# Prompt softmax of a hybrid decoder step: semaphores counted per head, and one move for both heads' turned weights where they fit in one bank

## The chip, the cores and the metric

The kernel runs on one core of one Trainium2 chip. The metric is device time in microseconds. Three runs of the kernel before gave 2883.32 to 2887.96 us, with a median of 2884.73 us.

## The reference

Two layers of a decoder step, for a prompt of 512 tokens and 8 sample requests of one token, each with 1024 cached tokens in pages of 128. Each layer normalizes, projects, attends, merges the branches by sigmoid gates and ends with a SwiGLU FFN. The attention has three kinds: native sparse attention (compressed, selected and window branch), stick-breaking, and forgetting attention (FoX). What the change touches is the masked softmax of the prompt:

```
def masked_softmax(s, mask):
    s = jnp.where(mask, s.astype(jnp.float32), NEG_INF)
    e = jnp.where(mask, jnp.exp(s - jnp.max(s, axis=-1, keepdims=True)), 0.0)
    return e / jnp.maximum(jnp.sum(e, axis=-1, keepdims=True), 1e-30)

p_c = masked_softmax(einsum('btghd,bngd->bghtn', qg, ck) * scale, c_mask);  o_c = einsum('bghtn,bngd->btghd', p_c, cv)
p_w = masked_softmax(einsum('btghd,bsgd->bghts', qg, k_win) * scale, w_mask); o_w = einsum('bghts,bsgd->btghd', p_w, v_win)
o = g[..., 0:1] * o_c + g[..., 1:2] * o_s + g[..., 2:3] * o_w
```

With 512 tokens, the selected and the window branch see every earlier token, so their weights form a causal triangle, as FoX's do. The compressed branch has 31 keys.

## The kernel before, in words

Each engine has its own program, and semaphores order them. A layer is `norm`, `project`, `compress`, `attend`, `merge`, `norm`, `ffn`. The change lies in `attend`, whose order is one list, `PLAN`, built by `in_order()` (from line 113). TensorE, VectorE and ScalarE each walk this list and skip what is not theirs; POOL walks `ITEMS` alone.

**Items.** `SOFT` has 14 units: for each of four pairs of query heads "cmp", "sel" and "win", then two units "fox". Each unit has four items, one for each block of 128 query rows (i = 0 to 3), so `ITEMS` has 56, numbered n. An item works on two heads, hh = 0 and 1. Its width w is 31 columns for "cmp" and (i + 1) x 128 otherwise. One item passes through these steps:

- `scores` (TensorE, lines 759 to 768): the scores of both heads go to PSUM banks 0 and 1. From n = 1 on it first waits for `exp_done` n, the exponentials of the item before.
- `scores` (VectorE, line 1700): the negated maximum of both heads.
- `exponentials` (ScalarE, line 1338): one operation for each head with the row sum as a by-product, into the buffer `Pb[:, n % 2]`; the semaphore rises after the second.
- `weigh` (VectorE, lines 1709 to 1713): mask, sum and clamp for "cmp" only, then the reciprocals of both heads' sums in one operation.
- POOL (lines 1492 and 1495): each head's weights times its reciprocal and its gate; `p_scaled` rises after the second head.
- `turn` (TensorE, line 582): for each head i + 1 transposes of 128 x 128 (one of 31 columns for "cmp") into bank 2. Head 0 waits for `p_scaled` and for VectorE's move of the item before; head 1 goes to the same columns of the bank and waits for ScalarE's move of head 0.
- `turn` (ScalarE, lines 1349 and 1351, head 0; VectorE, lines 1723 and 1725, head 1): the move from bank 2 to `PTb` in SBUF.
- `values` (TensorE, lines 800 and 802): after the fourth item of a unit, weights times values into bank 3.

The list has scores(n + 1), turn(n, 0), turn(n, 1), exp(n + 1), weigh(n + 1), and so on. On ScalarE the move of head 0 of item n is therefore ahead of the exponentials of item n + 1, and on VectorE the order is maximum of n + 1, move of head 1 of n, reciprocals of n + 1.

**Cached pages.** Between these parts `in_order()` spreads the work on the samples. Up to item 41 these are mostly the key pages: `turn_s` (four transposes, TensorE, also line 582, from the tile `units`), their move by VectorE (line 1788) and `score_s` (lines 938 and 939). Then come the samples' own softmax (lines 1796 to 1829, ScalarE 1388 to 1398) and, spread over the prompt items that are left and the stick-breaking heads, `value_s` (lines 1006 to 1009). SyncE loads the pages (`load_unit`, lines 541 and 557) into six slots in a fixed order; a slot is free when TensorE has read what was in it. The value pages of request b + 1 wait in this way for `value_s` of request b.

After the items follow the four stick-breaking heads; the first waits for the last exponentials and the last move of the softmax.

Of the kernel before, what the change touches and what calls it, by code (L numbers as in the profile page):

```python
# [13 lines left out]
P = 128  # L14
# [33 lines left out]
CONST, _c = {}, 0  # L48
# [36 lines left out]

STEPS = ([(("selk", b, 0), ("selk", b + 4, 0), j) for b in range(4) for j in range(2)]
# [89 lines left out]
def layer_counts():  # L176
# [9 lines left out]
             s_ps=items, nm_ready=items, exp_done=items, rr_ready=items, p_scaled=items, pt_ps=2 * items,  # L186
             pt_ev_a=items, pt_ev_d=items, pv_done=2 * len(SOFT), o_ev=8,
# [11 lines left out]
def build(nc, A, out):  # L199
# [4 lines left out]
    with ctx:  # L204
# [373 lines left out]
        def _(pe):  # L578
# [168 lines left out]
            def scores(l, n):  # L747
# [4 lines left out]
                if n >= 1:  # L752
                    pe.wait_ge(sems["exp_done"], at(pe, "exp_done", l, n))
# [16 lines left out]

            def turn(l, n, hh):

                u, i = ITEMS[n]
                if hh == 0:
                    pe.wait_ge(sems["p_scaled"], at(pe, "p_scaled", l, n + 1))
                    if n >= 1:
                        pe.wait_ge(sems["pt_ev_d"], at(pe, "pt_ev_d", l, n))
                else:
                    pe.wait_ge(sems["pt_ev_a"], at(pe, "pt_ev_a", l, n + 1))
                if SOFT[u][1] == "cmp":  # L780
                    last = tp(ps[0:NCP, 2, 0:P], Pb[:, n % 2, hh, 0:NCP], P)
                else:
                    for j in range(i + 1):
                        last = tp(ps[:, 2, j * P:(j + 1) * P], Pb[:, n % 2, hh, j * P:(j + 1) * P], P)
                last.then_inc(sems["pt_ps"], 1)

            def values(l, u):
                idx, br = SOFT[u]
                n = u * TT + TT - 1
                pe.wait_ge(sems["pt_ev_a"], at(pe, "pt_ev_a", l, n + 1))  # L790
                pe.wait_ge(sems["pt_ev_d"], at(pe, "pt_ev_d", l, n + 1))
# [17 lines left out]
            def stick(l, hd):  # L809
# [4 lines left out]
                if hd == 0:  # L814
                    pe.wait_ge(sems["exp_done"], at(pe, "exp_done", l, len(ITEMS)))
                    pe.wait_ge(sems["pt_ev_d"], at(pe, "pt_ev_d", l, len(ITEMS)))
# [405 lines left out]
        def _(act):  # L1222
# [107 lines left out]
            def exponentials(l, n):  # L1330
# [6 lines left out]
                for hh in range(2):  # L1337
                    last = fn(Pb[:, n % 2, hh, 0:w], ps[:, hh, 0:w], ACT.Exp, bias=nm[:, n % 2, hh:hh + 1], accum_out=sm[:, n % 2, hh:hh + 1])  # L1338
                last.then_inc(sems["exp_done"], 1)

            def turn(l, n, hh):
                if hh:
                    return
                u, i = ITEMS[n]
                act.wait_ge(sems["pt_ps"], at(act, "pt_ps", l, 2 * n + 1))
                if i == 0 and u >= 1:
                    act.wait_ge(sems["pv_done"], at(act, "pv_done", l, 2 * u))
                if SOFT[u][1] == "cmp":
                    fn(PTb[0:NCP, 0, 0, i * P:(i + 1) * P], ps[0:NCP, 2, 0:P], ACT.Copy).then_inc(sems["pt_ev_a"], 1)
                else:  # L1350
                    fn(PTb[:, 0, 0:i + 1, i * P:(i + 1) * P], ps[:, 2, 0:(i + 1) * P].rearrange("p (j c) -> p j c", c=P), ACT.Copy
                       ).then_inc(sems["pt_ev_a"], 1)
# [126 lines left out]
        def _(pool):  # L1479
            with pool.Fori(0, DEPTH) as i0:  # L1480
                l = in_layers(pool, i0)
                for n, (u, i) in enumerate(ITEMS):
# [13 lines left out]
                    last.then_inc(sems["p_scaled"], 1)  # L1496
# [62 lines left out]
        def _(dve):  # L1559
# [142 lines left out]
            def weigh(l, n):  # L1702
# [3 lines left out]
                dve.wait_ge(sems["exp_done"], at(dve, "exp_done", l, n + 1))  # L1706
                if SOFT[u][1] == "cmp":
                    m = CONST["cmp01"][0] + i * 32
                    link(v.tensor_tensor(Pb[:, b, :, 0:NCP], Pb[:, b, :, 0:NCP],
# [392 lines left out]
```

## Time and profile before

| | |
|---|---|
| median of 3 runs | 2884.73 us (2883.32 to 2887.96) |
| the profiled execution | 2888.6 us |
| its span, first to last instruction | 2886.8 us |
| mean granted TensorE clock | 0.935 of full speed |
| attention, layer 0 | from about 318 us to about 760 us |
| attention, layer 1 | from about 1728 us |

The profile gives, for each engine, the time in which it was busy, and for each instruction how long the engine had stood idle before it and which instruction of which engine ended that. An entry such as "PE ps L582 <- POOL ring L1495" reads: TensorE's instruction of line 582, which writes the tile ps, waited for POOL's instruction of line 1495, which writes the tile ring. `Pb` and `PTb` are parts of the tile ring, so the transposes of the prompt's weights are those of line 582 with input "cst,ring", and the page transposes those with "cst,units". The number of transposes in a row (x1 to x4) tells the row block i.

### The profile page before, as it was taken

Reading aid. Unit: us, or ns where it says so; the run is one execution under the profiler, and the core shown is the slowest. Engines: PE = TensorE matmul, PEld = TensorE weight load, DVE = VectorE, ACT = ScalarE, POOL = GpSimd, SP = SyncE. Lnnn points to the kernel's source line nnn. Section 1 sums busy time; section 2 is a strip of 40 time slices with the busy share of each in tenths; the row PEclk is TensorE's granted clock in tenths of the full one; section 3 lists DMA queues with packets and bytes.
Section 4 is the critical chain, followed back from the end, with each engine's and each line's share of the span. In section 5 each row is a group of like instructions: output and inputs, shape, how many; then the busy total and the mean of one; then the engine's idle time right before and its main releaser. Section 6 shows DMA issues by size and latency. Waiting matters only on the chain.

```text
span 2886.8 us, 43032 instructions
## 1 busy us (share of the span) xinstructions
PE 2584.5 (90%) x13546; PEld 1991.7 (69%) x13546; DVE 897.1 (31%) x1801; ACT 538.7 (19%) x1356; POOL 638.0 (22%) x564
## 2 busy tenths in 40 slices
PE   5997788877899999999999878888689999999997
PEld 4885544444588878888888664444357887888886
DVE  2203455421222432233131145552112334223412
ACT  1013222212222111110010232222141220111100
POOL 0000012111132424443300001121111242444431
PEclk8999789877999999999999998997789999999998
DMA  6242334245122212222514233341532222222120
GB/s 190 82 127 73 91 103 120 72 117 156 67 88 88 88 59 88 88 70 71 161 52 137 62 105 100 110 125 40 171 101 88 87 79 68 87 82 83 64 81 30
DMA packets 288295, 270.89 MB, mean 94 GB/s; under 512 B 50882, under 2 KB 249746, under 8 KB 287810
## 3 DMA queue, kind: packets, MB, share of 16 engines
q1 hardware_dynamic: 271266, 258.43, 29.2%
q10 hardware_dynamic: 16800, 9.61, 1.1%
q8 instruction: 119, 1.95, 0.3%
q14 instruction: 110, 0.90, 0.1%
HBM read 258.36 MB, written 17.97 MB: 96 GB/s over the span
## 4 chain that ended last, share of the span: by engine, by line
PE 77%; SPq 8%; issue 5%; DVE 5%; ACT 2%; POOL 1%; DMA 1%; ACTq 0%; DVEq 0%; POOLq 0%
PE ps L1042 32%; PE ps L1163 8%; PE ps L582 6%; PE ps L648 5%; PE ps L649 5%; SPq L557 3%; PE ps L938 3%; PE ps L863 2%; PE ps L802 2%; SPq L554 2%; POOL ring L1495 1%; PE ps L759 1%; PE ps L614 1%; PE ps L613 1%; PE ps L716 1%
## 5 line engine op out<-in xcount | busy, mean ns | idle before, releaser
L1495 POOL TENSOR_SCALAR ring<-ring,rr,gnat 128x31 f32<-128x31 f32 (+2 forms) x192 | 100.6, 534 | 1063.8 <-DVE rr L1713 1063.8
L1042 PE MATMUL ps<-hT,ring 128*128 128x260 f32 x1344 | 307.2, 386 | 8.2 <-DVE hT L1597 8.2
L1042 PEld LDWEIGHTS ps<-hT,ring 128*128 128x128 f32 x1344 | 258.2, 192 | 49.4 <-DVE hT L1597 9.0
L582 PE MATMUL ps<-cst,units 128*128 128x128 f32 x960 | 161.3, 302 | 61.2 <-ACT arena L1314 16.8
L1042 PE MATMUL ps<-hT,units 128*128 128x260 f32 x928 | 213.2, 382 | 0.0
L648 PE MATMUL ps<-hT,ring 128*128 128x260 f32 x672 | 202.4, 383 | 0.0
L649 PE MATMUL ps<-hT,ring 128*128 128x260 f32 x672 | 202.1, 382 | 0.0
L1042 PEld LDWEIGHTS ps<-hT,units 128*128 128x128 f32 x928 | 176.3, 190 | 27.1
L582 PEld LDWEIGHTS ps<-cst,units 128*128 128x128 f32 x960 | 114.6, 152 | 103.9 <-ACT arena L1314 38.0
L582 PE MATMUL ps<-cst,ring 128*128 128x128 f32 (+1 forms) x464 | 104.7, 314 | 75.9 <-POOL ring L1495 36.8
L1042 PE MATMUL ps<-arena,units 128*128 128x260 f32 x704 | 157.9, 382 | 0.0
L582 PEld LDWEIGHTS ps<-cst,ring 128*128 128x128 f32 (+1 forms) x464 | 54.9, 147 | 138.6 <-issue 72.5
L1042 PEld LDWEIGHTS ps<-arena,units 128*128 128x128 f32 x704 | 133.8, 190 | 20.5
L1788 DVE COPY arena<-ps 128x512 f32<-128x512 f32 x176 | 120.0, 687 | 88.4 <-PE ps L582 86.6
L649 PEld LDWEIGHTS ps<-hT,ring 128*128 128x128 f32 x672 | 127.7, 190 | 19.6
L648 PEld LDWEIGHTS ps<-hT,ring 128*128 128x128 f32 x672 | 126.3, 191 | 18.3
L1532 POOL TENSOR_TENSOR units<-ring 128x512 f32<-128x512 f32 x44 | 59.8, 1358 | 338.4 <-PE ps L1042 338.4
L1510 POOL TENSOR_TENSOR units<-ring 128x512 f32<-128x512 f32 x32 | 40.5, 1267 | 385.5 <-PE ps L1042 270.8
L1441 ACT ACTIVATE arena<-ps 128x260 f32<-128x260 f32 x132 | 51.1, 387 | 362.5 <-PE ps L1042 362.5
L1006 PE MATMUL ps<-units,arena 128*32 128x256 f32 x256 | 87.9, 506 | 33.2 <-DMA units<-in_cache_sb_kv 25.6
L1700 DVE TENSOR_REDUCE nm<-ps 128x2 f32<-128x256 f32 (+2 forms) x112 | 72.8, 650 | 140.4 <-PE ps L768 132.9
L1338 ACT ACTIVATE ring<-ps,nm 128x128 f32<-128x128 f32 (+2 forms) x224 | 100.3, 454 | 21.7 <-DVE nm L1700 21.2
(319 smaller groups left out, 4381.5 us busy)
## 6 DMA issues: line engine op xcount, KB each, us to landing
ring<-in_w_in SPq DMA_DIRECT2D x20, 2048.0 KB, 7.9
units<-in_cache_fox_kv SPq DMA_DIRECT2D x256, 128.0 KB, 2.2
units<-in_cache_sb_kv SPq DMA_DIRECT2D x256, 128.0 KB, 2.2
ring<-in_w_ffn_gate SPq DMA_DIRECT2D x22, 1024.0 KB, 5.4
ring<-in_w_ffn_up SPq DMA_DIRECT2D x22, 1024.0 KB, 8.0
ring<-in_w_ffn_down SPq DMA_DIRECT2D x16, 1408.0 KB, 6.2
units<-in_cache_nsa_cmp_kv SPq DMA_DIRECT2D x128, 128.0 KB, 2.6
units<-in_cache_nsa_sel_kv SPq DMA_DIRECT2D x256, 64.0 KB, 1.8
```

The costliest lines, as they stand in the source:

```text
L557: dma(slot[:, j * cols:(j + 1) * cols], rows(name)[l * NPOOL + pg][:, c0:c0 + cols]).then_inc(sem, 16)
L582: return nc.tensor.transpose(o, i, ident[0:n, 0:n])
L648: mm(ps[:, 2 * (i % 2), 0:H2], w[:, k, j * P:(j + 1) * P], hT[:, k, 0:H2], start=k == 0, stop=k == KD - 1)
L649: last = mm(ps[:, 2 * (i % 2) + 1, 0:H2], w[:, k, j * P:(j + 1) * P], hT[:, k, H2:T], start=k == 0, stop=k == KD - 1)
L938: mm(ps[lo, bank, :], qa, KT[0][:, i % 2, :], start=first, stop=True, skip_group_check=True).then_inc(sems["smm_a"], 1)
L1006: fox = mm(bank[64:96, 0:256], PTf[:, 4 * h + j, :], sf[:, j, :], start=h == 0 and j == 0, **sk)
L1042: last = mm(ps[:, bank, 0:H2], w[:, k, :], a[:, k, :], start=first and k == 0, stop=True, skip_group_check=True)
L1163: last = mm(ps[:, bank, 0:H2], w[:, k, :], x[k] if x is D2 else x[:, k, :], start=first and k == 0, stop=True, skip_group_check=True)
L1338: last = fn(Pb[:, n % 2, hh, 0:w], ps[:, hh, 0:w], ACT.Exp, bias=nm[:, n % 2, hh:hh + 1], accum_out=sm[:, n % 2, hh:hh + 1])
L1495: last = nc.gpsimd.tensor_scalar(p, p, one, gnat[:, i, c:c + 1], ALU.mult, ALU.mult)
L1700: v.tensor_reduce(nm[:, n % 2, :], ps[:, 0:2, 0:w], AX.X, ALU.max, negate=True).then_inc(sems["nm_ready"], 1)
L1788: v.tensor_copy(KT[s][:, i % 2, :], bank).then_inc(sems["kt_ev"], 1)
```

## The change

`exp_done`, `rr_ready` and `p_scaled` count heads instead of items. ScalarE raises `exp_done` after each head's exponentials. VectorE takes a reciprocal for each head by itself, except for "cmp", where it still takes both in one operation and raises the semaphore by two. POOL waits for each head's reciprocal and raises `p_scaled` after each head. TensorE's turn waits for the scaling of its own head.

A function `joint(n)` is true for "cmp" items and for i = 0 and 1. There both heads' turned weights lie side by side in bank 2, TensorE does not wait between them, and one instruction moves both: ScalarE's where n is even, VectorE's where n is odd. For i = 2 and 3 of the other branches head 0 is moved by ScalarE and head 1 by VectorE into and out of the same columns, as before. `MOVED_A` and `MOVED_D` hold how many moves each engine has made before item n. Before it overwrites or reads what was moved, TensorE waits for both counts.

```diff
+def joint(n):
+    u, i = ITEMS[n]
+    return i < 2 or SOFT[u][1] == "cmp"
+
+MOVED_A, MOVED_D = ([sum(not joint(m) or m % 2 == d for m in range(n)) for n in range(len(ITEMS) + 1)] for d in range(2))
...
+        def turned_weights(n, hh):
+            u, i = ITEMS[n]
+            cols = slice(i * P, (i + 1) * P)
+            if SOFT[u][1] == "cmp":
+                return PTb[0:NCP, :, 0, cols], ps[0:NCP, 2, 0:2 * P].rearrange("p (h c) -> p h c", h=2)
+            if joint(n):
+                return PTb[:, :, 0:i + 1, cols], ps[:, 2, 0:2 * (i + 1) * P].rearrange("p (h j c) -> p h j c", h=2, c=P)
+            return PTb[:, hh, 0:i + 1, cols], ps[:, 2, 0:(i + 1) * P].rearrange("p (j c) -> p j c", c=P)
...
 TensorE
+            def moved(l, n):
+                pe.wait_ge(sems["pt_ev_a"], at(pe, "pt_ev_a", l, MOVED_A[n]))
+                if MOVED_D[n]:
+                    pe.wait_ge(sems["pt_ev_d"], at(pe, "pt_ev_d", l, MOVED_D[n]))
             def turn(l, n, hh):
                 u, i = ITEMS[n]
-                if hh == 0:
-                    pe.wait_ge(sems["p_scaled"], at(pe, "p_scaled", l, n + 1))
-                    if n >= 1:
-                        pe.wait_ge(sems["pt_ev_d"], at(pe, "pt_ev_d", l, n))
-                else:
-                    pe.wait_ge(sems["pt_ev_a"], at(pe, "pt_ev_a", l, n + 1))
+                pe.wait_ge(sems["p_scaled"], at(pe, "p_scaled", l, 2 * n + hh + 1))
+                if hh == 0 and n >= 1:
+                    moved(l, n)
+                elif hh and not joint(n):
+                    pe.wait_ge(sems["pt_ev_a"], at(pe, "pt_ev_a", l, MOVED_A[n + 1]))
...
-                        last = tp(ps[:, 2, j * P:(j + 1) * P], Pb[:, n % 2, hh, j * P:(j + 1) * P], P)
+                        c = j + hh * (i + 1) * joint(n)
+                        last = tp(ps[:, 2, c * P:(c + 1) * P], Pb[:, n % 2, hh, j * P:(j + 1) * P], P)
...
 ScalarE
-                    last = fn(Pb[:, n % 2, hh, 0:w], ps[:, hh, 0:w], ACT.Exp, ...)
-                last.then_inc(sems["exp_done"], 1)
+                    fn(Pb[:, n % 2, hh, 0:w], ps[:, hh, 0:w], ACT.Exp, ...).then_inc(sems["exp_done"], 1)
             def turn(l, n, hh):
-                if hh:
+                if hh != joint(n) or joint(n) and n % 2:
                     return
-                act.wait_ge(sems["pt_ps"], at(act, "pt_ps", l, 2 * n + 1))
+                act.wait_ge(sems["pt_ps"], at(act, "pt_ps", l, 2 * n + hh + 1))
...
+                to, source = turned_weights(n, 0)
+                fn(to, source, ACT.Copy).then_inc(sems["pt_ev_a"], 1)
...
 POOL
-                    pool.wait_ge(sems["rr_ready"], at(pool, "rr_ready", l, n + 1))
-                    apart(pool)
                     for hh in range(2):
+                        pool.wait_ge(sems["rr_ready"], at(pool, "rr_ready", l, 2 * n + hh + 1))
+                        apart(pool)
...
-                    last.then_inc(sems["p_scaled"], 1)
+                        last.then_inc(sems["p_scaled"], 1)
...
 VectorE
-                dve.wait_ge(sems["exp_done"], at(dve, "exp_done", l, n + 1))
+                if SOFT[u][1] != "cmp":
+                    for hh in range(2):
+                        dve.wait_ge(sems["exp_done"], at(dve, "exp_done", l, 2 * n + hh + 1))
+                        v.reciprocal(rr[:, b, hh:hh + 1], sm[:, b, hh:hh + 1]).then_inc(sems["rr_ready"], 1)
+                    return
...
             def turn(l, n, hh):
-                if not hh:
+                if not hh or joint(n) and n % 2 == 0:
                     return
...
+                to, source = turned_weights(n, 1)
+                v.tensor_copy(to, source).then_inc(sems["pt_ev_d"], 1)
```

## Rows read from the trace of the kernel before

**Rows 1.** The page's first part: busy us, share of the span, instructions.

```profile
PE 2584.5 (90%) x13546; PEld 1991.7 (69%) x13546; DVE 897.1 (31%) x1801; ACT 538.7 (19%) x1356; POOL 638.0 (22%) x564
```

**Rows 2.** Windows: length, busy us (instructions) PE PEld DVE ACT POOL, clock, DMA share, GB/s.

```profile
318.00:599.00 281.00, 232.10 (x1359) 120.94 (x1355) 136.45 (x328) 69.89 (x256) 50.31 (x96) 0.88 0.30 88
1728.00:2008.00 280.00, 232.24 (x1374) 122.32 (x1377) 136.34 (x328) 71.30 (x261) 50.31 (x96) 0.88 0.30 90
```

**Rows 3.** Waits of TensorE, 318:599: us in total, times, longest.

```profile
PE ps L582 <- POOL ring L1495: 18.5, 22, 1.8
PE ps L582 <- ACT ring L1351: 11.6, 15, 2.9
PE ps L582 <- DVE arena L1788: 7.3, 8, 1.8
PE ps L582 <- ACT ring L1349: 2.2, 6, 0.4
...
PE ps L759 <- ACT ring L1338: 1.1, 2, 0.7
```

**Rows 4.** SyncE: waits in 318:760; timeline (start, us, instruction) of two issues.

```profile
SPq L557 <- PE ps L1009: 62.3, 2, 55.1
...
599.26 4.80 SPq L557 DMA_DIRECT2D units<-in_cache_nsa_sel_kv  x8
...
698.80 0.38 SPq L541 DMA_DIRECT2D units<-in_state_nsa_win_kv  x1
```

**Rows 5.** Waits of TensorE, 599:684.

```profile
PE ps L1006 <- DMA units<-in_cache_sb_kv: 10.8, 4, 4.4
```

**Rows 6.** TensorE: a group by form, 318:599, then turns in the timeline.

```profile
L582 PE MATMUL ps<-cst,ring 128*31 128x128 f32 x32 | 10.9, 341 | 10.5 <-POOL ring L1495 8.2 <-ACT ring L1349 2.2
...
470.28 0.30 PE L582 MATMUL ps<-cst,ring 128*31 128x128 f32 x1 [0.36 <-ACT ring L1349]
...
478.70 0.29 PE L582 MATMUL ps<-cst,ring 128*31 128x128 f32 x1 [0.88 <-POOL ring L1495]
...
560.02 0.69 PE L582 MATMUL ps<-cst,ring 128*128 128x128 f32 x2 [2.92 <-ACT ring L1351]
```

**Rows 7.** Timeline, all engines, 558:562.

```profile
558.36 0.94 DVE L1700 TENSOR_REDUCE nm<-ps 128x2 f32<-128x768 f32 x1
558.46 1.15 ACT L1388 ACTIVATE arena<-arena,s 32x1025 f32<-32x1025 f32 x1 [11.63 <-DVE s L1806]
...
561.13 1.22 PE L759 MATMUL ps<-PT 64*128 64x512 f32 x2 [0.42 <-ACT ring L1338]
```

**Rows 8.** Waits of VectorE, 318:599.

```profile
DVE rr L1713 <- ACT ring L1338: 0.4, 2, 0.2
```

**Rows 9.** Groups by form, POOL and VectorE, 318:704: count, busy us, mean ns.

```profile
L1495 POOL TENSOR_SCALAR ring<-ring,rr,gnat 128x512 f32<-128x512 f32 x16 | 12.2, 770 | 31.4 <-DVE rr L1713 31.4
L1495 POOL TENSOR_SCALAR ring<-ring,rr,gnat 128x31 f32<-128x31 f32 x32 | 11.9, 381 | 397.0 <-DVE rr L1713 397.0
L1495 POOL TENSOR_SCALAR ring<-ring,rr,gnat 128x384 f32<-128x384 f32 x16 | 10.5, 663 | 36.1 <-DVE rr L1713 36.1
L1495 POOL TENSOR_SCALAR ring<-ring,rr,gnat 128x256 f32<-128x256 f32 x16 | 8.8, 557 | 49.7 <-DVE rr L1713 49.7
...
L1713 DVE RECIPROCAL rr<-sm 128x2 f32<-128x2 f32 x56 | 8.9, 160 | 2.3 <-ACT ring L1338 1.3 <-DVE sm L1712 0.2
L1725 DVE COPY ring<-ps 128x512 f32<-128x512 f32 x10 | 6.9, 692 | 25.4 <-PE ps L582 25.2
...
L1725 DVE COPY ring<-ps 128x256 f32<-128x256 f32 x10 | 4.2, 423 | 10.1 <-PE ps L582 9.7
```

**Rows 10.** Timeline: POOL and VectorE at 323, ScalarE at 470.

```profile
323.32 0.75 POOL L1495 TENSOR_SCALAR ring<-ring,rr,gnat 128x31 f32<-128x31 f32 x2 [322.88 <-DVE rr L1713]
323.35 0.26 DVE L1750 TENSOR_SCALAR pc<-pc,s 64x63 f32<-64x63 f32 x1
...
469.96 0.27 ACT L1349 ACTIVATE ring<-ps 31x128 f32<-31x128 f32 x1 [3.54 <-PE ps L582]
```

More of the change, by code:

```diff
@@ L185, in layer_counts @@
              kt_ps=ksteps, kt_ev=ksteps, kt_ea=CMPT, cs_ps=16, cs_ev=8, cvs_ps=2, cvs_ev=2,
-             s_ps=items, nm_ready=items, exp_done=items, rr_ready=items, p_scaled=items, pt_ps=2 * items,
-             pt_ev_a=items, pt_ev_d=items, pv_done=2 * len(SOFT), o_ev=8,
+             s_ps=items, nm_ready=items, exp_done=2 * items, rr_ready=2 * items, p_scaled=2 * items, pt_ps=2 * items,
+             pt_ev_a=MOVED_A[-1], pt_ev_d=MOVED_D[-1], pv_done=2 * len(SOFT), o_ev=8,
              sbz_ps=4, sb_ln=4, sb_sp=4, sbc_ps=4, sb_w=4, sb_pv=4,
@@ L789, in values @@
                 n = u * TT + TT - 1
[L790 to L791 removed]
+                moved(l, n + 1)
                 if idx >= 1 and br in ("cmp", "fox"):
@@ L1337, in exponentials @@
                 for hh in range(2):
-                    last = fn(Pb[:, n % 2, hh, 0:w], ps[:, hh, 0:w], ACT.Exp, bias=nm[:, n % 2, hh:hh + 1], accum_out=sm[:, n % 2, hh:hh + 1])
-                last.then_inc(sems["exp_done"], 1)
+                    fn(Pb[:, n % 2, hh, 0:w], ps[:, hh, 0:w], ACT.Exp, bias=nm[:, n % 2, hh:hh + 1], accum_out=sm[:, n % 2, hh:hh + 1]
+                       ).then_inc(sems["exp_done"], 1)
             def turn(l, n, hh):
-                if hh:
+                if hh != joint(n) or joint(n) and n % 2:
                     return
                 u, i = ITEMS[n]
-                act.wait_ge(sems["pt_ps"], at(act, "pt_ps", l, 2 * n + 1))
-                if i == 0 and u >= 1:
+                act.wait_ge(sems["pt_ps"], at(act, "pt_ps", l, 2 * n + hh + 1))
+                if i <= 1 and u >= 1:
                     act.wait_ge(sems["pv_done"], at(act, "pv_done", l, 2 * u))
[L1348 to L1352, printed above, removed]
+                to, source = turned_weights(n, 0)
+                fn(to, source, ACT.Copy).then_inc(sems["pt_ev_a"], 1)
             def values(l, u):
@@ L1705, in weigh @@
                 b = n % 2
[L1706 to L1713 removed]
+                if SOFT[u][1] != "cmp":
[3 more added lines that the diff above has]
+                    return
+                dve.wait_ge(sems["exp_done"], at(dve, "exp_done", l, 2 * n + 2))
+                m = CONST["cmp01"][0] + i * 32
+                link(v.tensor_tensor(Pb[:, b, :, 0:NCP], Pb[:, b, :, 0:NCP],
+                                     cst[:, m:m + NCP].rearrange("p (a c) -> p a c", a=1).broadcast_to([P, 2, NCP]), ALU.mult))
+                link(v.reduce_sum(sm[:, b, :], Pb[:, b, :, 0:NCP], AX.X))
+                link(v.tensor_scalar(sm[:, b, :], sm[:, b, :], 1e-30, None, ALU.max))
+                v.reciprocal(rr[:, b, :], sm[:, b, :]).then_inc(sems["rr_ready"], 2)
             def turn(l, n, hh):
[L1716 removed]
+                if not hh or joint(n) and n % 2 == 0:
                     return
@@ L1719, in turn @@
                 dve.wait_ge(sems["pt_ps"], at(dve, "pt_ps", l, 2 * n + 2))
-                if i == 0 and u >= 1:
+                if i <= 1 and u >= 1:
                     dve.wait_ge(sems["pv_done"], at(dve, "pv_done", l, 2 * u))
-                if SOFT[u][1] == "cmp":
-                    v.tensor_copy(PTb[0:NCP, 1, 0, i * P:(i + 1) * P], ps[0:NCP, 2, 0:P]).then_inc(sems["pt_ev_d"], 1)
-                else:
-                    v.tensor_copy(PTb[:, 1, 0:i + 1, i * P:(i + 1) * P], ps[:, 2, 0:(i + 1) * P].rearrange("p (j c) -> p j c", c=P)
-                                  ).then_inc(sems["pt_ev_d"], 1)
+                to, source = turned_weights(n, 1)
+                v.tensor_copy(to, source).then_inc(sems["pt_ev_d"], 1)
             def sp(l, hd):
```

12 lines of the change are left out of this document (4 added, 8 removed).

## The prediction

> **What bounds the kernel now.** I read the page first: TensorE has a matmul in it for 90% of the span and no other engine for more than 31% [rows 1]. So a change to the softmax can bring time only where TensorE stands still for it. The attention stage begins at 318 us in layer 0 and at 1728 us in layer 1. In the two stretches 318:599 and 1728:2008 TensorE is busy 232.10 of 281 and 232.24 of 280 us [rows 2]. Both layers look alike, so I work out layer 0 and double it.
>
> The waits of TensorE in 318:599 name the causes [rows 3]: 18.5 us for POOL's scaling of the weights (22 times), 11.6 + 2.2 us for ScalarE's move of head 0 (15 and 6 times), 7.3 us for VectorE's moves of cached keys, 1.1 us for the exponentials. Layer 1 has 18.3, 11.6, 2.2, 7.3 and 1.1.
>
> What sets the end differs after 599 us. SyncE issues the value pages of requests 1 to 7. The first of them goes out at 599.26, the last before its next stop at 698.80, and SyncE's waits in 318:760 say that it waited for a value matmul twice, 55.1 us ahead of 599 and 7.2 us after 699 [rows 4]; between the two it issues back to back. TensorE waits for the stick-breaking pages there, 10.8 us in 599:684 [rows 5]. A softmax that is quicker between 599 and about 683 us makes TensorE wait longer for pages. What is won before 599, on the contrary, lets value_s(0, 0) free its slots earlier and moves SyncE's whole row of issues with it: I count it in full. So the sum runs over items 0 to 46 of each layer.
>
> **The change part by part.**
>
> *Second head turned without waiting for the first head's move* (the 36 joint items of a layer: "cmp", and row blocks i = 0 and 1). It takes away TensorE's wait for ScalarE between the two heads. In the compressed items that is all of the 2.2 us [rows 3]; one such is the 0.36 us at 470.28 [rows 6]. Of the 11.6 us of the other items I went through the 15 rows: five with one or two transposes are joint (0.47, 0.45, 0.48, 0.45, 0.45 = 2.3 us), nine with three or four transposes aren't (6.4 us, these stay), and one is the 2.92 us at 560.02 [rows 6]. That last one is joint and its wait goes, but the stall does not: VectorE starts the maximum of the next item only at 558.36, ScalarE is in the cached softmax from 558.46 for 1.15 us, and the next scores at 561.13 wait for the exponentials behind both [rows 7]. TensorE will stand before the scores instead; I count nothing. Where other work stands between the two heads (as the four page transposes after 478.70) the wait has no label now, and I count nothing either. Gain 2.2 + 2.3 = 4.5 us.
>
> *Scaling signalled per head.* Turn(n, 0) starts after one POOL operation where it waited for two. It could be more, since the reciprocal no longer needs the second exponential; but in 318:599 the reciprocal waited for ScalarE only 0.4 us in all [rows 8]: VectorE comes late to it, behind its moves of keys. So each wait can lose at most one POOL operation: 381 ns for 31 columns, 557 for 256, 663 for 384, 770 for 512 [rows 9]. The 22 waits of 18.5 us [rows 3]:
> compressed items, nine with 8.2 us in all [rows 6], none under 0.49 (0.88 at 478.70): 9 x 0.38 = 3.4.
> i = 1, four of 0.26, 0.81, 0.80 and 0.85: 0.26 + 3 x 0.56 = 1.9.
> i = 2 and 3, nine from 0.26 to 1.76 with 7.5 us in all, each cut at 0.66 or 0.77: 5.8.
> Gain 11.1 us. The second head's transposes are then behind POOL's second operation, which ends when it ended before: the old start of turn(n, 0), so hardly a wait.
>
> *One move where two stood.* On odd joint items VectorE moves both heads: 512 columns for 256 at i = 1 (0.692 for 0.423 us [rows 9]), and 256 for 128 in compressed items, by the same slope 0.13 us more. Eight of each before 599: 8 x 0.27 + 8 x 0.13 = 3.2 us more, ahead of the next item's reciprocal, in the queue that is late for it. On even ones VectorE is free of its move, and ScalarE's is wider and now waits for both heads; the next item's exponentials stand behind it. Between the heads of an even item lies up to 1.2 us of other TensorE work. Cover: VectorE reaches the reciprocal late anyway.
>
> *Reciprocals.* 31 more by 0.16 [rows 9] is 5.0 us of VectorE before 599, against 16 moves of 128 columns that it gives up on even items (0.29 by the slope, 4.6 us). They could delay the moves of keys for which TensorE waits 7.3 us. Bounds of both VectorE costs together: 0 to 8.2 us per layer on the path. I take 3, near the moves' 3.2, because the reciprocal of head 1 comes when VectorE formerly gave its only one.
>
> *More waits on TensorE's queue*: one for the second head's scaling, and a pair in place of the single one for the moves. ScalarE's move ends at 470.23 and TensorE starts at 470.28 [rows 6, 10], so a whole hand-over with its wait is 0.05 us. One more wait at a stalled start costs between nothing and that: 22 x 0.05 = 1.1. I take 1. Behind it on the queue stand page transposes and key scores, whose inputs have landed: SyncE waited for TensorE in this stretch, not the reverse.
>
> Sum per layer: 4.5 + 11.1 - 3 - 1 = 11.6 us, with the bounds 15.6 and 15.6 - 8.2 - 1.1 = 6.3. Two layers: 23 us (13 to 31). The profiled execution took 2888.6 us (span 2886.8 and 1.8 around it); 2865.5 after. The median of the three runs is 3.9 us lower, 2884.7, so 2861.5; I say 2861.
>
> A rule of the Trainium skill speaks against half of the change. "Perfetto Trace Analysis", Optimizing Scalar/DVE Operations: where these engines aren't saturated but cause bubbles elsewhere, breaking up instructions may let work complete sooner. That is the per-head signal; joining the moves is the opposite. Here VectorE is busy 136.45 of 281 us [rows 2] and is late all the same. By the rule the joint moves lose 3.2 us and split ones would be the better form; the row on TensorE's 4.5 us between the heads speaks for joining, and I go by it.
>
> **Rivals.**
>
> *A. VectorE eats it.* The loop is limited by VectorE's queue and all of its bounds fall due: 2 x 6.3 = 13 us, time 2872. For: the reciprocal waits for ScalarE hardly ever [rows 8]. Against: even items relieve VectorE by about as much as the reciprocals add.
>
> *B. More than counted.* The twenty handshakes of joint items without a label, and the parts of POOL waits above my cap: labelled joint waits and all POOL waits are 18.5 + 2.2 + 2.3 = 23 us per layer, 46 in both, 2839. With it goes the clock: its mean is 0.88 in 318:599 [rows 2], and a shorter pause may keep it at the higher level. Against: the cap comes from a queue that the change does not empty.
>
> *C. Nothing.* The stall moves in every item, as at 560.02, to the scores behind the exponentials or to VectorE's key moves; 2884. For: the long 2.92 us wait does just that. Against: the 1.1 us now spent before the scores in 47 items [rows 3]; the exponentials are mostly done when TensorE comes.
>
> *D. Slower: the reciprocal of head 1 blocked by POOL.* It is now issued while POOL scales head 0, and formerly never was. If VectorE is held until that operation ends, each of the 31 items loses one POOL operation on VectorE's queue (0.56 to 0.77, and 0.45 at i = 0 by the slope between the rows [rows 9]; mean 0.61): 19 us per layer, and the second head's scaling starts only after it, so that the 7.7 us won at i = 1 to 3 go as well. Of the 11.6 us 3.9 are left: 2 x (19 - 3.9) = 30 us, 2915. It decides once the block outlasts the slack that even items give. Against: at 323.35 a VectorE scaling of 63 columns ran beside a POOL operation begun at 323.32 and was through in 0.26 us, while POOL's two operations took 0.75 [rows 10]; held to the end of the first it would have needed about 0.6. "SBUF — State Buffer", Who interferes with whom, of the Trainium skill has such a lock between VectorE and GpSimd for VectorE's two-port modes and for two SBUF inputs; a reciprocal of one column isn't named there, and no row of this trace shows one beside POOL.
>
> **How the numbers follow.** Forecast's case (2846 to 2867) 0.60; A and what lies between it and the forecast (2867 to 2879) 0.17; B 0.06; C 0.11; D 0.06. The range of 8 in 10 takes the first two and part of C: 2845 to 2882. A measurement of this kernel can tell 0.2%, 5.8 us, from no change. Faster by more: 0.60 + 0.17 + 0.06 = 0.83; within: 0.11; slower: 0.06.
>
> **What would show it.** Right: in 318:599 TensorE's wait for ScalarE's moves falls from 13.8 to about 6.4 us per layer, all at i = 2 and 3, with none in compressed items, and the 2.9 us at 560 stands before the scores instead; its wait for POOL from 18.5 to 7 or 8; the first value page of request 1 is issued at about 587 in place of 599; from there to the stick-breaking part the DMA waits grow. VectorE has 80 more reciprocals and 72 fewer moves of weights between it and ScalarE. Wrong: POOL waits as long as before (VectorE later by as much), waits before the scores or for the key moves that grow by more than 7 us per layer, or reciprocals longer than 0.2 us, which would be D.

## The result, and the profile after it

The changed kernel takes 2860.0 us (median of four runs, 2855.9 to 2863.3) against 2885.3 for the kernel before beside it: ratio 0.9915, 95% interval 0.9903 to 0.9928, 25 us less where 23 were forecast. The time is right, the way to it only in part: the waits of TensorE with a label shrank by 4 us in layer 0 and not by 11.6, and the rest is TensorE's own busy time, in good part by a higher granted clock, which the sum had not counted.

The profiled execution after took 2855.9 us (span 2854.0). The page's first part answers to [rows 1]:

```profile
PE 2556.9 (90%) x13546; PEld 1983.5 (69%) x13546; DVE 899.6 (32%) x1845; ACT 531.6 (19%) x1320; POOL 638.8 (22%) x564
```

VectorE has 44 instructions more (80 more reciprocals, 36 fewer moves) and ScalarE 36 fewer.

To compare stretches whose ends are the same events, I cut from TensorE's first cached compressed scores to SyncE's issue of the first value page of request 1, and on to the end of the value pages. First the kernel before, then the changed one (layer 0, layer 1, layer 0's value part each); columns as in [rows 2].

```profile
320.85:599.26 278.41, 230.92 (x1343) 120.28 (x1343) 135.41 (x326) 69.89 (x256) 50.31 (x96) 0.87 0.30 88
1728.35:2002.55 274.20, 227.13 (x1343) 118.75 (x1343) 135.22 (x326) 70.00 (x256) 50.31 (x96) 0.88 0.30 90
599.26:734.45 135.19, 102.69 (x681) 59.77 (x679) 22.10 (x43) 30.12 (x57) 17.12 (x16) 0.79 0.57 166
```

```profile
319.19:581.68 262.49, 219.34 (x1345) 117.06 (x1343) 136.10 (x342) 67.01 (x240) 50.32 (x96) 0.90 0.32 94
1708.85:1971.52 262.67, 220.72 (x1345) 117.65 (x1343) 136.02 (x342) 67.02 (x240) 50.32 (x96) 0.89 0.32 94
581.68:715.91 134.23, 93.82 (x680) 56.24 (x677) 22.81 (x49) 29.66 (x55) 17.12 (x16) 0.83 0.56 167
```

I call the first stretch the key part. It lost 15.9 us in layer 0 and 11.5 in layer 1, and the value part 1.0, though TensorE's busy time there fell by 8.9 us. In the key part of layer 0 TensorE has the same matmuls but is busy 11.6 us less, at a mean clock of 0.90 for 0.87. The mean is of two levels, 1 being 2.4 GHz and 0.5 being 1.2 GHz.

The trace has the stretches at either level. Laid over TensorE's matmuls they give 62.4 us of busy time at the lower level before and 45.4 after. As an estimate I count half of that time as clock and the rest of the busy time as TensorE's rows, its work at full clock. The estimate holds in that the same code then has the same rows in both layers, 199.7 and 200.0 us before, though it is busy 3.8 us longer in one of them; after they are 196.6 and 196.7. So the 15.9 us of layer 0 are 4.3 of waits, 3.1 of rows and 8.5 of clock; the 11.5 of layer 1 are 5.1, 3.3 and 3.1.

TensorE's waits in the key part of layer 0, against [rows 3] (us in total, times, longest; L599, L776 and L960 were L582, L759 and L938):

```profile
PE ps L599 <- POOL ring L1514: 10.2, 13, 1.6
PE ps L599 <- DVE arena L1808: 10.2, 11, 2.1
PE ps L776 <- ACT ring L1360: 7.1, 5, 3.5
PE ps L599 <- ACT ring L1371: 7.1, 9, 2.3
PE ps L960 <- DVE arena L1808: 2.6, 8, 0.3
```

For POOL 18.5 us became 10.2, for ScalarE's moves 13.8 became 7.1. But before the scores, behind the exponentials, 1.1 became 7.1, and for VectorE's key moves (both lines; the second had 0.8 us in the kernel before) 8.1 became 12.8. Net: 41.5 to 37.2 us, which is the 4.3 above.

### The profile page after: what moved, and what is told of

Its sections match the earlier page's. It is cut to its first block, busy times and chain, and to the rows that moved or that the text cites. A ratio compares the mean times of both kernels' runs of the same rounds, so it can differ in the third digit from the quotient of the medians.

```text
span 2854.0 us, 43454 instructions
## 1 busy us (share of the span) xinstructions
PE 2556.9 (90%) x13546; PEld 1983.5 (69%) x13546; DVE 899.6 (32%) x1845; ACT 531.6 (19%) x1320; POOL 638.8 (22%) x564
## 3 DMA queue, kind: packets, MB, share of 16 engines
q1 hardware_dynamic: 271266, 258.43, 29.5%
## 4 chain that ended last, share of the span: by engine, by line
PE 79%; DVE 6%; issue 6%; SPq 5%; ACT 2%; DMA 1%; POOL 0%; ACTq 0%; DVEq 0%; POOLq 0%
PE ps L1064 33%; PE ps L1185 8%; PE ps L599 6%; PE ps L665 5%; PE ps L666 5%; PE ps L960 3%; SPq L574 3%; PE ps L776 2%; PE ps L885 2%; PE ps L824 2%; PE ps L733 1%; PE ps L630 1%; PE ps L631 1%; SPq L571 1%; DVE arena L1808 1%
## 5 line engine op out<-in xcount | busy, mean ns | idle before, releaser
L599 PE MATMUL ps<-cst,units 128*128 128x128 f32 x960 | 156.7, 296 | 61.1 <-DVE arena L1808 20.5
L1064 PEld LDWEIGHTS ps<-hT,units 128*128 128x128 f32 x928 | 176.3, 190 | 27.1
L599 PEld LDWEIGHTS ps<-cst,units 128*128 128x128 f32 x960 | 113.1, 150 | 102.6 <-DVE arena L1808 37.9
L599 PE MATMUL ps<-cst,ring 128*128 128x128 f32 (+1 forms) x464 | 96.6, 306 | 41.7 <-ACT ring L1371 20.6
L599 PEld LDWEIGHTS ps<-cst,ring 128*128 128x128 f32 (+1 forms) x464 | 54.5, 147 | 92.9 <-issue 57.7
```

Of the source, the lines that this page charges most:

```text
L599: return nc.tensor.transpose(o, i, ident[0:n, 0:n])
L1064: last = mm(ps[:, bank, 0:H2], w[:, k, :], a[:, k, :], start=first and k == 0, stop=True, skip_group_check=True)
```

## The experiments

A table first; each kernel stands against the kernel before run beside it. The waits are TensorE's in the key part of layer 0, summed from rows like those above. The diffs below leave out conditions that have become constant and the counts that follow from the edit.

| kernel | us | ratio, 95% interval | key part | POOL | ScalarE's moves | before scores | key moves |
|---|---|---|---|---|---|---|---|
| before | 2885 | 1 | 278.4 | 18.5 | 13.8 | 1.1 | 8.1 |
| the change | 2860.0 | 0.9915 (0.9903 to 0.9928) | 262.5 | 10.2 | 7.1 | 7.1 | 12.8 |
| e1 signals alone | 2864.5 | 0.9931 (0.9916 to 0.9946) | 267.4 | 10.7 | 15.1 | 1.1 | 8.8 |
| e2 joining alone | 2888.0 | 1.0008 (0.9999 to 1.0017) | 279.4 | 20.8 | 6.2 | 6.3 | 11.6 |
| e3 late reciprocals | 2865.8 | 0.9930 (0.9917 to 0.9943) | 262.6 | 10.6 | 6.9 | 6.1 | 12.9 |
| e4 items 0 to 46 | 2865.6 | 0.9932 (0.9920 to 0.9944) | 263.0 | 8.9 | 7.1 | 7.1 | 12.9 |
| e5 the change again | 2862.0 | 0.9921 (0.9907 to 0.9934) | 262.9 | 8.9 | 7.1 | 7.1 | 12.9 |
| e6 moves on ScalarE | 2856.4 | 0.9904 (0.9889 to 0.9920) | 262.8 | 7.7 | 7.1 | 10.4 | 13.1 |
| e7 moves on VectorE | 2853.3 | 0.9894 (0.9879 to 0.9909) | 256.4 | 12.2 | 7.1 | 4.1 | 13.1 |
| e8 reciprocals first | 2841.7 | 0.9855 (0.9840 to 0.9870) | 257.1 | 4.4 | 5.3 | 11.0 | 12.0 |
| e9 e8 and e7 | 2839.6 | 0.9838 (0.9824 to 0.9851) | 257.3 | 7.2 | 5.3 | 8.1 | 12.7 |
| e10 before, reciprocals first | 2863.5 | 0.9927 (0.9913 to 0.9940) | 267.4 | 13.0 | 11.8 | 4.2 | 7.3 |
| e11 e8 without joining | 2843.8 | 0.9855 (0.9839 to 0.9870) | 259.2 | 5.3 | 12.5 | 5.1 | 7.9 |
| e12 items 47 to 55 | 2894.8 | 1.0032 (1.0021 to 1.0043) | 279.1 | 21.9 | 13.9 | 1.1 | 7.3 |

The second table splits the profiled execution of each kernel as above: both layers' key parts together, in us against the kernel before.

| kernel | waits | rows | clock | in all |
|---|---|---|---|---|
| the change | -9.5 | -6.4 | -11.6 | -27.5 |
| e1 signals alone | -11.1 | +0.3 | -10.1 | -20.9 |
| e2 joining alone | +6.7 | -4.2 | -0.3 | +2.2 |
| e3 late reciprocals | -10.0 | -6.5 | -6.6 | -23.1 |
| e4 items 0 to 46 | -10.6 | -7.3 | -6.8 | -24.6 |
| e5 the change again | -10.8 | -7.3 | -7.5 | -25.7 |
| e6 moves on ScalarE | -5.5 | -6.0 | -16.5 | -28.0 |
| e7 moves on VectorE | -10.3 | -4.8 | -19.4 | -34.4 |
| e8 reciprocals first | -15.6 | -2.9 | -19.2 | -37.7 |
| e9 e8 and e7 | -15.5 | -3.3 | -19.3 | -38.1 |
| e10 before, reciprocals first | -9.6 | +5.2 | -15.6 | -20.0 |
| e11 e8 without joining | -20.8 | +3.9 | -17.3 | -34.2 |
| e12 items 47 to 55 | +6.2 | +2.2 | -2.8 | +5.6 |

The key parts of e8 to e11 have 14 matmuls a layer more (1357 for 1343), since their end lies a little later in the order; their rows can be compared only with each other. The clock column is of one execution each: the change and e5, the same kernel, are 4 us apart in it.

**Each half alone (e1, e2).**

```diff
 def joint(n):
-    return i < 2 or SOFT[u][1] == "cmp"
+    return False
```

> The per-head signals alone (exponential, reciprocal, POOL's scaling); both heads' turned weights go one after the other through the bank in two moves, as in the kernel before. Theory of the prediction (signals are the larger part, 11 of 15.6 us a layer, less the reciprocals on VectorE): 2867 to 2871 us, 14 to 18 us faster than before; TensorE's wait for POOL in the key part of layer 0 near 10 us, its wait for ScalarE's moves unchanged near 14 us. Rival, joining is what matters: 2878 or more. Rival, splitting is the better form and the wider moves lose: 2857 or less.

The signals alone give 20 us of the 25, a little more than expected. The rows of e1 (ScalarE's move is L1375 there, POOL L1518):

```profile
PE ps L601 <- ACT ring L1375: 15.1, 21, 2.9
PE ps L601 <- POOL ring L1518: 10.7, 15, 1.7
PE ps L601 <- DVE arena L1812: 8.1, 9, 1.8
...
PE ps L778 <- ACT ring L1364: 1.1, 2, 0.7
```

Only POOL's row changed by more than 1.3 us against [rows 3]: this half does what it says. The two layers' key parts are 20.9 us shorter, 11.1 by waits and 10.1 by the clock.

```diff
-                       ).then_inc(sems["exp_done"], 1)
+                    if hh:
+                        last.then_inc(sems["exp_done"], 2)
...
-                        last.then_inc(sems["p_scaled"], 1)
+                        if hh:
+                            last.then_inc(sems["p_scaled"], 2)
```

The reciprocal is one instruction for both heads again, and POOL and TensorE wait once an item.

> Joining alone: both heads turned into one bank and moved at once in the 36 joint items, all signals once an item as before. Theory of the prediction: 4.5 us a layer less at most 1.6 for the wider moves on VectorE, so 2876 to 2881 us, 4 to 9 us faster than before; wait for POOL unchanged near 18 us, wait for ScalarE's moves near 7. Rival, joining is what matters: 2868 or less. Rival, the wider moves make VectorE late: 2885 or more.

No gain; the third theory's number (2885 or more) is the one that came. The wait between the heads is gone in the joint items, 13.8 to 6.2 us, and has moved on:

```profile
PE ps L599 <- POOL ring L1517: 20.8, 23, 2.0
PE ps L599 <- DVE arena L1816: 9.2, 11, 2.1
PE ps L776 <- ACT ring L1361: 6.3, 5, 3.5
PE ps L599 <- ACT ring L1373: 6.2, 9, 1.7
PE ps L961 <- DVE arena L1816: 2.4, 8, 0.3
```

Before the scores 5.2 us more, for key moves 3.5 more, for POOL 2.3 more: 11 against the 7.6 removed. What joining does bring is in the rows, some 2 us a layer. The prediction saw this shift in one place, the 2.92 us at 560.02 [rows 6, 7], and there it is in the changed kernel (start, us, engine; idle before in brackets):

```profile
540.66 0.94 DVE L1719 TENSOR_REDUCE nm<-ps 128x2 f32<-128x768 f32 x1
540.76 1.15 ACT L1407 ACTIVATE arena<-arena,s 32x1025 f32<-32x1025 f32 x1 [10.65 <-DVE s L1826]
...
543.17 2.08 PE L776 MATMUL ps<-PT 64*128 64x512 f32 x4 [3.55 <-ACT ring L1360]
```

**The reciprocal per head (e3).**

```diff
-                if SOFT[u][1] != "cmp":
-                    for hh in range(2):
-                        dve.wait_ge(sems["exp_done"], at(dve, "exp_done", l, 2 * n + hh + 1))
-                        v.reciprocal(rr[:, b, hh:hh + 1], sm[:, b, hh:hh + 1]).then_inc(sems["rr_ready"], 1)
+                dve.wait_ge(sems["exp_done"], at(dve, "exp_done", l, 2 * n + 2))
+                v.reciprocal(rr[:, b, :], sm[:, b, :]).then_inc(sems["rr_ready"], 2)
```

> Joining and POOL's signal per head, but exponentials and reciprocals signalled and done once an item as before. Theory of the prediction (VectorE comes late to the reciprocal, so that the first head's earlier exponential buys nothing): 2857 to 2863 us, the same as the change. Rival, the early reciprocal matters: 2866 or more, half-way back. Rival, the additional reciprocals load VectorE: 2855 or less, and shorter waits for key moves than the change's 12.8 us.

2865.8 lies between the two expectations, and its interval overlaps that of e5, so the time does not tell them apart. The profile does for the key part of layer 0: 262.6 us as in the change, POOL's wait 10.6 us as in the change; layer 1 is 4.2 us longer than the change's, by the clock (28.8 us lost to its lower level for 24.0). So the per-head exponential and reciprocal add 4 us at most against e5, 6 against the first runs of the change, and perhaps nothing; the gain is POOL's own signal, though no run has that one without joining.

**Where it counts (e4, e12, e5).**

```diff
-    return i < 2 or SOFT[u][1] == "cmp"
+    return n < 47 and (i < 2 or SOFT[u][1] == "cmp")
```

The signals likewise: per head for n < 47, both at the second head for the others. e12 is the same with n >= 47.

> The change in items 0 to 46 of each layer alone; items 47 to 55 (the last window item and both fox pairs) have the form of before. Theory of the prediction (SyncE's row of page issues sets the end from there, nothing is won after item 46): 2857 to 2864 us, within 3 us of the change. Rival, the whole attention gains evenly: 9 of 56 items, 4 us of 25 lost, and the wide items of fox more than their share, 2865 to 2870.

> The change in items 47 to 55 of each layer alone; items 0 to 46 have the form of before. Theory of the prediction (what is won after item 46 turns into waits for value pages): 2881 to 2886 us, within 3 us of before, with the wait for stick-breaking pages in 599:684 of layer 0 longer than 10.8 us. Rival (the whole attention gains evenly): 4 us or more, 2879 or less.

> The changed kernel once more, unaltered, as the measure for the runs beside it. All theories: 2857 to 2864 us, 21 to 28 us faster than before.

e4 keeps 20 us, where e5 has 23. It is 3.6 us above e5, with overlapping intervals, 2 us over its expected band and at the lower edge of the rival's (2865 to 2870), so its time does not decide. Its profile speaks for the theory: without the change in its last nine items the value part of layer 0 takes 133.1 us (582.82 to 715.90), where the change takes 134.2 and e5 136.2. e12 is slower than before by 9 us (6 to 12), which neither theory allowed. Its last nine items bring nothing (value part 135.0 us for 135.2), and the stick-breaking pages are waited for longer (TensorE, 599:735 of e12; 10.8 in [rows 5]):

```profile
PE ps L1033 <- DMA units<-in_cache_sb_kv: 16.6, 5, 4.7
```

But its first 47 items were meant to be as before and are not: POOL's wait there is 21.9 us. A stalled turn of the kernel before, then of e12:

```profile
477.82 0.74 POOL L1495 TENSOR_SCALAR ring<-ring,rr,gnat 128x31 f32<-128x31 f32 x2 [3.57 <-DVE rr L1713]
```

```profile
468.86 0.74 POOL L1521 TENSOR_SCALAR ring<-ring,rr,gnat 128x31 f32<-128x31 f32 x2 [4.30 <-DVE rr L1748]
469.83 0.29 PE L601 MATMUL ps<-cst,ring 128*31 128x128 f32 x1 [1.50 <-POOL ring L1521]
```

In the kernel before POOL ends at 478.56 and TensorE starts at 478.70 [rows 6], 0.14 us later; in e12 POOL ends at 469.60 and TensorE starts at 469.83, 0.23 later. In the key part of layer 0 all 22 starts of the turns behind POOL in the kernel before have the first value within 0.01, and 21 of 22 in e12 have the second. e12 and e2 share with the change the pair of waits for the moves behind the one for POOL, where the kernel before has a single one: that one more wait costs 0.09 us each time TensorE has stood. e12 and e2 also raise POOL's counter by two, but the change raises it by one and is as late (below, under the hardware). 22 stalls x 0.09 are 2.0 us a layer, which is most of the growth of POOL's wait in e2 (2.3) and over half of it in e12 (3.4). In all e12 waits 2.9 and 3.3 us longer in the two key parts, and its rows take 1.3 and 0.9 more; in layer 0 3.5 us less clock hides most of it, in layer 1 (279.2 for 274.2 us) nothing does. Where the waits beyond the 2.0 and the longer rows come from stays open.

**Whose moves (e6, e7).**

```diff
-                if hh != joint(n) or joint(n) and n % 2:
+                if hh != joint(n):
...
-                if not hh or joint(n) and n % 2 == 0:
+                if not hh or joint(n):
```

The first pair of lines is ScalarE's, the second VectorE's, and this is e6; e7 has "hh != joint(n) or joint(n)" and "not hh".

> The change, but all 36 joint moves of a layer are made by ScalarE, in place of every second one by VectorE. Joining alone gave nothing, because in the key part of layer 0 the waits before the scores grew from 1.1 to 6.3 us and those for key moves from 8.1 to 11.6. Theory 1 (VectorE's wider moves in the queue ahead of key moves and reciprocals are what takes joining's gain back): key-move waits fall to 8 or 9 us, POOL waits too, and the time is 2852 to 2858 us. Theory 2 (the later and wider moves stand ahead of the exponentials on ScalarE, and TensorE stands before the scores): twice as many such items, waits before the scores 10 us or more, 2863 to 2872 us.

> The change, but all 36 joint moves of a layer are made by VectorE. Theory 1 (VectorE's queue takes joining's gain back): key-move waits 16 us or more in the key part of layer 0, POOL waits 13 or more, 2870 to 2880 us. Theory 2 (ScalarE's moves ahead of the exponentials do): the waits before the scores go back toward 1 us, and the time is 2855 to 2862 us.

Both are at or below the change; e7 is faster than e5 by 0.27% (intervals touch). Theory 1 fails: with all 36 wide moves on VectorE the wait for key moves is 13.1 us, with none on it 13.1 as well. It does not depend on who moves the weights. Theory 2 has the waits right (before the scores 10.4 with ScalarE moving, 4.1 with VectorE), but e6's time is not worse: POOL's wait falls to 7.7 where VectorE is free, and though the two key parts still wait 5.3 us longer than e5's, the clock takes 9.0 less. e6's time lies in theory 1's band without theory 1's cause.

```profile
PE ps L599 <- POOL ring L1515: 12.2, 16, 1.6
PE ps L599 <- DVE arena L1809: 10.5, 11, 2.4
PE ps L599 <- ACT ring L1372: 7.1, 9, 2.3
PE ps L776 <- ACT ring L1361: 4.1, 2, 3.5
PE ps L961 <- DVE arena L1809: 2.6, 8, 0.3
```

These are e7's waits. Its windows show the clock by itself:

```profile
321.35:577.75 256.40, 213.79 (x1345) 114.86 (x1343) 140.86 (x358) 62.92 (x224) 50.36 (x96) 0.93 0.33 95
1705.26:1967.08 261.82, 220.12 (x1345) 117.22 (x1343) 140.94 (x358) 62.91 (x224) 50.38 (x96) 0.90 0.32 94
```

The same instructions and nearly the same waits in both layers (36.5 and 35.6 us over these five rows), but 5.4 us between them: TensorE is busy 6.3 us longer in layer 1, at 0.90 for 0.93. That much two passes over the same code can differ. e7's lead over e5 in the two key parts is clock too: 11.9 us, with waits and rows 3.0 us longer.

**VectorE late at the reciprocal (e8, e10).** The prediction held that what remains of POOL's wait is VectorE, behind its key moves. In the changed kernel:

```profile
462.38 1.29 DVE L1808 COPY arena<-ps 128x512 f32<-128x512 f32 x2 [1.61 <-PE ps L599]
...
463.10 0.18 ACT L1360 ACTIVATION_READ_ACCUMULATOR ring<-ps,nm 128x1 f32 x1
...
463.58 0.21 DVE L1732 TENSOR_TENSOR ring<-ring,cst 128x62 f32<-128x62 f32 x1
...
464.71 0.74 POOL L1514 TENSOR_SCALAR ring<-ring,rr,gnat 128x31 f32<-128x31 f32 x2 [3.19 <-DVE rr L1736]
...
465.31 0.29 PE L599 MATMUL ps<-cst,ring 128*31 128x128 f32 x1 [0.50 <-POOL ring L1514]
```

The exponentials end at 463.28; VectorE is in two key moves until 463.6, and TensorE waits 0.50 us at the end of the chain. The written-out order puts one other step between an item's exponentials and its reciprocals in 32 of 55 items, in 16 of them a page transpose with VectorE's move. Giving "exp" no weight in it puts them next to each other in all:

```diff
-        weight = [{"stick": 3, "behind": 3, "stick_v": 3, "sp": 0}.get(p[0], 1) for p in a]
+        weight = [{"stick": 3, "behind": 3, "stick_v": 3, "sp": 0, "exp": 0}.get(p[0], 1) for p in a]
```

> The change, with nothing put between an item's exponentials and its reciprocals in the written-out order, so that page transposes and VectorE's key moves no longer stand ahead of the reciprocals. Theory of the prediction (VectorE comes late to the reciprocal behind its key moves, and that is what remains of POOL's wait): POOL waits in the key part of layer 0 fall from 10.2 to 6 us or less, VectorE waits for ScalarE before the reciprocal instead, time 2848 to 2855 us. Rival (the key moves are then late by as much, since VectorE stands for the exponential ahead of them): 2860 to 2868 us, key-move waits over 15 us.

> The kernel before, with the reciprocals directly behind the exponentials in the written-out order and nothing of the change. Theory (VectorE comes late to the reciprocal, in the kernel before as in the change): POOL waits in the key part of layer 0 from 18.5 to 12 or 13 us, 2865 to 2874 us. Rival (the order pays only with signals per head, since a single reciprocal must wait for both exponentials): 2880 or more.

```profile
PE ps L776 <- ACT ring L1360: 11.0, 9, 3.6
PE ps L599 <- DVE arena L1808: 9.7, 10, 2.1
PE ps L599 <- ACT ring L1371: 5.3, 8, 2.1
PE ps L599 <- POOL ring L1514: 4.4, 10, 0.6
PE ps L960 <- DVE arena L1808: 2.3, 7, 0.3
```

These are e8's waits, and POOL's is 4.4. Time: 20 us below e5, more than expected; the key moves are not later. About half of it is in the key parts (257.1 and 257.8 us), the rest in the value parts and after, where the order moved too (value part of layer 0: 128.6 us for 134.2). In the key parts it is mostly clock: against e5 the waits are 4.8 us shorter, the rows 4.4 longer with their 28 more matmuls, and 11.7 is clock. Alone, on the kernel before (e10), the same edit gives 21 us, nearly as much as the whole change (23 to 25), and POOL's wait falls to 13.0:

```profile
PE ps L582 <- POOL ring L1495: 13.0, 18, 1.3
PE ps L582 <- ACT ring L1351: 10.3, 14, 2.9
PE ps L582 <- DVE arena L1788: 6.8, 8, 1.6
PE ps L759 <- ACT ring L1338: 4.2, 4, 1.8
PE ps L582 <- ACT ring L1349: 1.5, 4, 0.4
```

Here too 15.6 of the 20.0 us of the key parts are clock, and 9.6 waits. The edit also shifts other steps of the order by an item here and there, so that not every microsecond need be the reciprocals'.

**Together (e9, e11).** e9 is e8 with e7's moves, e11 is e8 with e1's joint(n).

> The change with the reciprocals directly behind the exponentials and all 36 joint moves on VectorE. Theory (the two repairs work on different waits: the order on POOL's, 10.2 to 4.4 us, VectorE's moves on those before the scores, 7.1 to 4.1): they add, 2832 to 2838 us, and the wait before the scores in the key part of layer 0 falls from 11.0 to 8 us or less. Rival (with the reciprocals early, the scores wait for the exponentials because ScalarE itself is late by its own row of waits): the same as the order alone, 2839 to 2845.

> Signals per head and the reciprocals directly behind the exponentials, without joining. Theory (joining takes 7 us of waits for ScalarE's moves away and gives most of it back before the scores and the key moves): 2841 to 2848 us, 0 to 6 us slower than with joining. Rival (the earlier scaling makes joining worth its full 4.5 us a layer): 2849 or more.

e9 is the fastest kernel, 2839.6 us, 45 below before, but cannot be told from e8: the rival's band is the one it hit. The wait before the scores fell to 8.1 as said, and POOL's rose from 4.4 to 7.2. Without joining (e11) the time is the same within the intervals, as the theory had it: joining removes 7.2 us of waits for ScalarE's moves and puts 5.9 before the scores and 4.1 before key moves, and the rows get 3.4 us a layer shorter.

## Why the prediction came out right

The 25 us fit the forecast's 23, but not for its reason alone. The sum held that the change can bring time only where TensorE stands still, and put 11.6 us a layer there. The waits gave 4.3 and 5.1 us in the profiled execution, 5.5 and 5.3 in e5. The rest, TensorE's rows and its clock, was in no term of the sum, and that it filled the gap is luck.

**SyncE's row sets the end after 599.** Right. The first value page of request 1 goes out at 581.68, and the value part keeps its length (135.19 and 134.23) although TensorE needs 8.9 us less in it. What is won in it turns into waits for pages, 22.9 us in 581.68:684 for the 10.8 of [rows 5]:

```profile
PE ps L1028 <- DMA units<-in_cache_sb_kv: 22.9, 5, 6.1
```

**Scaling per head, 11.1 us a layer.** Right as to what carries the change, and somewhat large as a wait: 18.5 became 10.2, 8.3 less (7.8 in e1). At i = 1 to 3 it went from 10.2 to 2.6 us, as good as the 7.7 of the sum. The step that was mis-sized is the compressed items: 3.4 forecast, 0.6 measured (changed kernel, by form; [rows 6] has the one of before).

```profile
L599 PE MATMUL ps<-cst,ring 128*31 128x128 f32 x32 | 9.2, 318 | 7.6 <-POOL ring L1514 7.6
```

My sum subtracted an operation from every wait as if TensorE came at the same time as before. That it comes earlier by what the step before has won, while the chain of key move, reciprocal and scaling stands where it stood, is my reading. Two runs fit it: e1, without joining, has the same 7.6 us, and in e8, with the reciprocals first, this form waits 3.1 us.

**The earlier exponential and reciprocal buy nothing.** Supported by e3 in the key part. In the changed kernel VectorE makes most pairs of reciprocals back to back, without a wait between them:

```profile
492.51 0.43 DVE L1728 RECIPROCAL rr<-sm 128x1 f32<-128x1 f32 x2
492.85 1.09 POOL L1514 TENSOR_SCALAR ring<-ring,rr,gnat 128x256 f32<-128x256 f32 x2 [4.13 <-DVE rr L1728]
```

**Joining, 4.5 us a layer.** The wait went nearly as forecast (13.8 to 7.1, where 6.4 was named), and what is left is all at the wider items, none in compressed ones. But the step "I count nothing" for the stall that moves to the scores, made for the one place at 560, had to be made for five places, and the key moves came on top. Joining alone is worth nothing (e2), with the signals 2 to 5 us (e1 against e5 and the change, e11 against e8), within the intervals. What it does bring with them is in TensorE's busy time, 225.3 to 219.3 us (e1 to the change) and 221.9 to 217.5 (e11 to e8): 3.1 and 3.5 us of these are rows, the others clock. By form, clock included, TensorE's turns of 31 columns go from 10.4 to 9.2 us and the wider ones from 31.1 to 29.5 (e1 to the change); the page transposes, which joining does not touch, only from 58.6 to 57.3. The sum had no term for that.

**Wider moves and more reciprocals on VectorE, 3 us.** The cost was put in the wrong place. Key-move waits grew by 4.7 us, yet e6 and e7 show that the wider moves have no part in it, and e3 that the reciprocals have none. They come with joining, whoever moves: 7.3 to 8.8 us without it, 11.6 to 13.1 with it. That TensorE reaches the page transposes sooner and VectorE's copies set the pace would fit, but no run tests it. The other cost is in part ScalarE's, whose wide moves stand before the next exponentials: 10.4 us with all on ScalarE, 4.1 with none. Together 10.7 us a layer where I took 3 and bounded 8.2: the sum of waits fails here, and what I had named as a sign against the forecast, more than 7 us of growth before the scores or at the key moves, was there if the two are taken together (6.0 + 4.7), while the time came out.

**More waits on TensorE's queue, 1 us.** 0.09 us each rather than 0.05, at 13 stalls rather than 22: 1.2 us.

**Clock.** Counted only under rival B. It was 8.5 of 15.9 us in the profiled execution's layer 0 and 3.1 of 11.5 in its layer 1; in e5, the same kernel, 6.7 of 15.5 and 0.8 of 10.1. So the total was right because the clock and the shorter rows gave back what the moved stalls took. Whether shorter pauses raised the clock is not shown, but chance alone is unlikely. Its lower level cost 27.1 to 31.2 us in the six key parts in which TensorE waits 47 us or more (before, e2, e12), 15.9 to 28.8 in the 22 others, and 19.1 to 22.8 in all eight with the reciprocals first. e7's two layers (15.9 and 23.1 us) show how far it moves without any cause in the code.

**Readings.** The 11.6 us of waits for ScalarE that I gave for layer 1 are those up to the first value page, which goes out at 2002.55 there; in 1728:2008 they are 12.3. The sum used layer 0 and doubled it, so it does not change.

**The rivals.** A (VectorE eats it): no, e3, e6 and e7. B: its clock was there, its 46 us of waits were not. C (nothing): right for joining alone, wrong for the change. D (the head-1 reciprocal held by POOL): no. Where ScalarE is late in the changed kernel, the second reciprocal begins while POOL works, and takes 0.16 us, as those beside nothing do:

```profile
530.04 1.09 POOL L1514 TENSOR_SCALAR ring<-ring,rr,gnat 128x256 f32<-128x256 f32 x2 [4.72 <-DVE rr L1728]
530.14 0.16 DVE L1728 RECIPROCAL rr<-sm 128x1 f32<-128x1 f32 x1 [0.29 <-ACT ring L1360]
```

"SBUF — State Buffer", Who interferes with whom, of the Trainium skill frees instructions with at most one SBUF input outside the two-port modes from the lock, and does not name the reciprocal on either side; these rows show no lock for it.

The rule of the Trainium skill that I weighed ("Perfetto Trace Analysis", Optimizing Scalar/DVE Operations: on engines that aren't saturated, broken-up instructions may let work complete sooner) fits these runs better than my choice did: the split signal gave 20 us, the joined moves nothing by themselves and 2 to 5 us with it.

## What to carry to other kernels

Where several engines hand one item round, signal each half as it is ready, and keep what the slowest link waits for out of the way: moving unrelated steps from between the exponentials and the reciprocals gave as much as the signals, and the two added up (21 and 20 us alone, 41 together). A wait that is removed between two halves of an item comes back at the next hand-over unless the engine behind that is early, so cost a removed wait by the next thing that is late in every item, not in the longest one. And split a result into waits, rows and clock before calling a sum of waits right: here the clock was as large as the waits, and larger where the order was changed. The untried next steps: the waits for the moves put ahead of the one for POOL on TensorE's queue, and fewer or shorter key moves, which now lead with 12 us a layer. POOL's signal without joining, and moving each head from the shared bank as soon as it is turned, were not tried either.

## What the runs showed of the hardware

One more wait behind one at which TensorE has stood is 0.09 us, even where it was met long before: start after POOL's end 0.13 or 0.14 us with one wait behind it, 0.23 with two. One kernel has both values: in e6 and e7 one of the two move counters still stands at nothing in items 2 and 3, so that its wait is left out, and the seven starts there read 0.13, nearly all later ones 0.23. Three starts of a joint item's second head (e7, e8, e9), with no wait behind POOL's, read 0.02 or 0.03. The change has the same: at 461 us POOL's pair runs from 460.77 for 0.74, so its first operation ends at about 461.14, and TensorE starts 0.24 later.

```profile
460.77 0.74 POOL L1514 TENSOR_SCALAR ring<-ring,rr,gnat 128x31 f32<-128x31 f32 x2 [3.35 <-DVE rr L1736]
461.38 0.29 PE L599 MATMUL ps<-cst,ring 128*31 128x128 f32 x1 [1.14 <-POOL ring L1514]
```

The second surprise is the clock: the granted mean of a 260 us stretch of the same code was 0.93 in one layer and 0.90 in the other (e7), and that was worth 5.4 us, as much as a gain that one would look for. Between kernels it moved with the order of the work: 0.87 and 0.88 before, 0.91 in both layers of e8 and e9.
